# A hybrid decoder step on one core: tokens scaled when their pieces begin, four weight chunks in the idle ring, constants and counts in another order, 8 pieces ahead

## The chip, the core and the metric

The kernel runs on one core of one Trainium2 chip. The metric is the device time of one execution in microseconds; the median of several executions is compared. All data are 32-bit floats.

## What is computed

The reference is one inference step of a one-layer decoder for 1024 prompt tokens and 8 sample tokens of width 1024. Cut to what matters here:

```python
def step(y, pos):                                   # y: (tokens, 1024)
    qr, kr, vr, gr, qs, ks, vs = split(rms_norm(y, norm1_g) @ w_in)   # w_in: 1024 x 2816
    o_ret, state = retention(rotate(qr, pos), rotate(kr, pos), vr)    # 4 heads, blocks of 128 tokens, carried state
    o_swa = sliding_attention_with_sinks(qs, ks, vs)                  # 8 heads, window 128
    h = y + concat(norm(o_ret) * silu(gr), o_swa) @ w_out             # 1024 x 1024
    x = rms_norm(h, norm2_g)
    s = (x @ peer_w_q) . sub_keys                   # 8 heads x 2 halves x 128 keys
    idx, gates = top 16 of the 16 x 16 sums of the two top 16s, softmax
    a = gelu(peer_u[idx] . x) * gates               # 128 rows of 1024 per token
    return rms_norm(h + a @ peer_v[idx], final_g)
```

Each of the 1032 tokens takes 128 rows of `peer_uv`, a table of 16384 rows of 8 KB (u and v side by side). Fetching them is most of what the kernel moves: 1032 x 128 x 8 KB is 1.08 GB.

## The kernel before

**Blocks and ticks.** The 1024 prompt tokens are 8 blocks `b` of 128. For each block a loop of 128 units (`TICKS`) fetches one row per token and unit: GpSimd issues an indirect DMA (`fetch`, L577) of 1 MB into one of 8 slots of `ring`; VectorE forms the dot product with the token (`expert_dot`, L1648), ScalarE the weight (`weigh`, L1144, and scaled diagonals, L963), TensorE adds gate times row for a pair of units (`add_pair`, L899), and that frees the two slots (`used`) for the next fetches. The work for the next block ("front": `mixing`, then `picking`) is laid between these units by Python generators on each engine: each yields the tick at which its next part is due, and `advance` emits it there. Each engine runs its own list in order; only semaphores tie them.

**Ahead of the loop.** Block 0 has no loop to hide in. First `project_first` multiplies block 0 by the 8 weight chunks of `w_in` (L615), fed by `load_w` (L350) into three buffers in `ring`. Then `mixing(0)` and `picking(0)` run, with `key_weights` between them: the product of `peer_w_q` and the sub keys, from 16 loads `load_wqT` (L359), in TensorE's rows as L659. Then come the top-16 choices on VectorE (`rank`, `choose`, `number`), in two halves of the heads. `number` for a half ends with a wait for ScalarE's exponential of the gates (`best_exp`, L1115), and `move_picks` on SyncE's queue (L442, L443) then carries the choices to where GpSimd reads them. GpSimd's first fetch waits for that.

**Pieces.** The input projection of tokens 128 to 1031 is cut into 128 pieces `q` (`PIECES`): 16 column chunks for block 1, then 16 for blocks 2 and 3, then 16 for blocks 4 to 7 and the samples. A piece is `project_late` (8 matmuls, L642 and L639) on TensorE, `late_out` on ScalarE (copy with the token's scale into one of four staging places), `store_late` on SyncE (L375, 88 KB to `proj_scratch`), and `load_late` (L368, 704 KB of weights into one of three buffers, issued when the piece three chunks earlier is done). The first `AHEAD` = 14 pieces stand ahead of the loop, the others in it, at `late_tick(q)`:

```python
    if q < EARLY:
        return 1 + (q - AHEAD) * 4 // 3
```

`load_columns(b)` (L447, L448) brings a block's projected columns and its rotation table back; VectorE's `rotate` (L1311) waits for both at tick 20.

**Tokens.** The projection needs transposed tokens times the gain of the norm (`gain`, L1254), and a scale per token from its sum of squares (`count`, L1260; `load_x`, L344). Before, the transposed tokens of blocks 4 to 7 and the samples are loaded to `xT_kept` in the upper half of `ring` (L490, L492), scaled there, stored to DRAM (`xT_scratch`, L499) and loaded again in the loop (L391). The upper half of `ring` then takes `w_out` for block 0 (`wo_first`, L505).

**SyncE's queue** issues all the direct DMAs in the order written, waits included. The constants (`loads`, L494, 17 of them) stand behind all eight weight chunks and `xT_kept`.

## Time and profile before

| | us |
|---|---|
| median of 3 executions | 3050.13 |
| lowest, highest | 3045.28, 3050.16 |
| the profiled execution | 3047.14 |
| its span in the trace | 3045.3 |
| first fetch of an expert row | 200.5 |
| TensorE, VectorE, ScalarE, GpSimd busy | 74%, 67%, 34%, 39% |
| moved by the DMA engines | 1217 MB, mean 400 GB/s |

The span is read in two parts: up to the first fetch, and the loop behind it. The share of DMA is the mean busy share of the core's 16 DMA engines; GB/s says what they moved in that time, and with small packets a full share moves less.

### The profile page before, as it was taken

The page shows a single profiled execution, that of the slowest core. Times are in us where ns is not written, and L with a number is a line of the kernel's source. Part 1 is how long each engine was busy: PE and PEld are TensorE (multiplying, and loading weights), DVE is VectorE, ACT ScalarE, POOL GpSimd, SP SyncE. Part 2 cuts the span into 40 slices and gives each one's busy share as a digit, 9 for nine tenths or more (in the row PEclk, how much of TensorE's full clock was granted, in tenths as well). Part 3 has the DMA queues.
Part 4 walks back from the last instruction along what each step waited for, and adds up shares of the span by engine and source line. Part 5 has one row for each costly group of instructions (what it writes and reads, how often), then busy time and mean ns, then how long its engine had stood idle before and what let it go on. Part 6 is the DMA issues. An engine that isn't in the chain of part 4 may idle for free.

```text
span 3045.3 us, 29029 instructions
## 1 busy us (share of the span) xinstructions
PE 2251.6 (74%) x8794; PEld 961.4 (32%) x8794; DVE 2031.1 (67%) x4937; ACT 1029.3 (34%) x3215; POOL 1199.2 (39%) x1052
## 2 busy tenths in 40 slices
PE   7887968877698867866687577856785577778564
PEld 5565723544245532232222122212221122211111
DVE  2365546775468655787558865797569765886875
ACT  1322523334233343323432353233432343333322
POOL 0012343333444334434444444444444444444542
PEclk9898988998899988967798778977897789879867
DMA  8569999999999999999999999999999999999998
GB/s 312 220 244 406 403 409 416 407 421 399 421 419 419 411 416 420 417 381 411 420 421 412 407 421 421 418 403 421 421 415 408 412 418 421 408 410 421 416 408 333
DMA packets 194286, 1217.47 MB, mean 400 GB/s; under 512 B 25480, under 2 KB 44336, under 8 KB 59600
## 3 DMA queue, kind: packets, MB, share of 16 engines
q0 software_dynamic: 148608, 1082.20, 86.1%
q1 hardware_dynamic: 45520, 133.41, 11.4%
q8 instruction: 69, 1.13, 0.1%
q14 instruction: 89, 0.73, 0.1%
HBM read 1193.59 MB, written 21.54 MB: 399 GB/s over the span
## 4 chain that ended last, share of the span: by engine, by line
DMA 38%; PE 33%; DVE 16%; issue 6%; ACT 3%; POOL 3%; SPq 0%; DVEq 0%; POOLq 0%; ACTq 0%
DMA ring<-in_peer_uv,idxg 33%; PE ps L899 14%; PE ps L861 8%; DVE ring L1648 7%; PE ps L642 5%; DMA proj_scratch<-wo 3%; POOL ring L577 3%; ACT ring L963 2%; PE ps L842 1%; DMA wo<-in_w_in 1%; DVE proj L1502 1%; DVE proj L1495 1%; PE ps L659 1%; PE ps L615 1%; DVE proj L1553 1%
## 5 line engine op out<-in xcount | busy, mean ns | idle before, releaser
L577 POOL DMA_INDIRECT ring<-in_peer_uv,idxg x1024 | 1183.0, 1155 | 1607.5 <-PE ps L899 1359.2
L899 PE MATMUL ps<-ring 128*64 128x512 f32 x4096 | 1240.5, 737 | 662.2 <-ACT ring L963 660.0
L1648 DVE SCALAR_TENSOR_TENSOR ring<-ring,xlo 128x1024 f32<-128x1024 f32 x512 | 627.1, 1225 | 415.1 <-DMA ring<-in_peer_uv,idxg 400.1
L1648 DVE SCALAR_TENSOR_TENSOR ring<-ring,xhi 128x1024 f32<-128x1024 f32 x512 | 626.8, 1224 | 395.3 <-DMA ring<-in_peer_uv,idxg 384.8
L899 PEld LDWEIGHTS ps<-ring 128*64 128x64 f32 x4096 | 290.3, 158 | 1457.0 <-ACT ring L963 984.3
L1144 ACT ACTIVATE small<-small 128x2 f32<-128x2 f32 x512 | 104.7, 204 | 1638.5 <-DVE ring L1648 1627.8
L642 PE MATMUL ps<-wo 128*128 128x176 f32 x1792 | 304.1, 327 | 39.4 <-ACT wo L963 14.1
L642 PEld LDWEIGHTS ps<-wo 128*128 128x128 f32 x1792 | 279.9, 197 | 103.8 <-issue 82.3
L963 ACT ACTIVATE ring<-gdiag,small 128x64 f32<-128x64 f32 x1024 | 301.6, 342 | 16.7
L963 ACT ACTIVATE gdiag<-fold,gateg 128x64 f32<-128x64 f32 x1024 | 294.5, 336 | 1.5
L861 PE MATMUL ps<-keyw,work 128*128 128x512 f32 (+1 forms) x576 | 267.0, 608 | 1.1 <-ACT work L963 1.1
L861 PEld LDWEIGHTS ps<-keyw,work 128*128 128x128 f32 (+1 forms) x576 | 98.7, 180 | 168.3 <-issue 166.8
L1502 DVE FIND_INDEX8 proj<-proj 128x8 uint32<-128x128 f32 (+3 forms) x432 | 135.3, 333 | 0.0
L1495 DVE MAX8 proj<-proj 128x8 f32<-128x128 f32 (+3 forms) x432 | 109.5, 323 | 12.7 <-ACT proj L963 12.2
L842 PE MATMUL ps<-wo,work 128*128 128x512 f32 x224 | 109.6, 623 | 0.0
L963 ACT ACTIVATE wo<-ps,small 128x176 f32<-128x176 f32 (+2 forms) x115 | 47.9, 418 | 145.1 <-PE ps L642 78.2
L586 POOL COPY idxg<-stage 128x64 uint32<-128x64 uint32 x16 | 7.4, 461 | 199.2 <-DMA stage<-moving 199.2
L1144 ACT ACT_TABLE_LOAD x64 | 82.1, 1283 | 1.1
L1510 DVE MATCH_REPLACE8 proj<-proj 128x128 f32<-128x128 f32 (+3 forms) x216 | 66.9, 321 | 0.0
L842 PEld LDWEIGHTS ps<-wo,work 128*128 128x128 f32 x224 | 40.2, 195 | 72.0 <-issue 72.0
L1311 DVE TENSOR_TENSOR work<-proj,qsT 128x256 f32<-128x256 f32 x64 | 22.8, 421 | 55.4 <-DMA small<-in_swa_sinks 36.7
L1559 DVE TENSOR_TENSOR proj<-proj 128x256 f32<-128x256 f32 (+1 forms) x144 | 51.3, 417 | 0.1
(199 smaller groups left out, 1521.6 us busy)
## 6 DMA issues: line engine op xcount, KB each, us to landing
wo<-in_w_in SPq DMA_DIRECT2D x48, 704.0 KB
ring<-in_peer_uv,idxg POOLq DMA_INDIRECT x1024
wo<-in_w_out SPq DMA_DIRECT2D x4, 4096.0 KB, 17.5
ring<-in_w_in SPq DMA_DIRECT2D x8, 1408.0 KB, 6.9
proj_scratch<-wo SPq DMA_DIRECT2D x112, 88.0 KB
proj<-proj_scratch SPq DMA_DIRECT2D x7, 1408.0 KB
ring<-in_wqT SPq DMA_DIRECT2D x16, 512.0 KB, 7.0
h<-in_x_prompt SPq DMA_DIRECT2D x9, 512.0 KB, 9.1
```

The source lines that it names most:

```text
L577: nc.gpsimd.indirect_dma_start(row[r], None, A["peer_uv"], bass.IndirectOffsetOnAxis(ap=experts, axis=0)).then_inc(ld_row[r], 16)
L642: mm = nc.tensor.matmul(o, late_T(n, k), w[:, k, :], start=(k == 0), stop=(k == KC - 1))
L842: mm = nc.tensor.matmul(F[2 + n][0:rows, :], lhsT, weights[:, k, n * 512:(n + 1) * 512], start=(k == 0), stop=(k == KC - 1))
L861: mm = nc.tensor.matmul(F[n][0:rows, :], xT[:, k * P:k * P + rows], keyw[:, k, n * 512:(n + 1) * 512], start=(k == 0), stop=(k == KC - 1))
L899: mm = nc.tensor.matmul(acc[side * HP:(side + 1) * HP, n * 512:(n + 1) * 512], row_u[r][:, 0:HP], row_v[r][:, n * 512:(n + 1) * 512], star ...
L963: return nc.scalar.activation(o, i, ACT.Copy, **kw_)
L1144: me.did(nc.scalar.activation(gel[:, r:r + 2], dot[:, r:r + 2], ACT.Gelu))
L1495: me.did(nc.vector.max(v16(j)[:, r8 * 8:r8 * 8 + 8], rowsof(j)))
L1502: me.did(nc.vector.max_index(i16(j)[:, r8 * 8:r8 * 8 + 8], v16(j)[:, r8 * 8:r8 * 8 + 8], rowsof(j)))
L1510: me.did(nc.vector.match_replace(rowsof(j), v16(j)[:, 0:8], rowsof(j), TAKEN))
L1559: me.did(tt(o3, o3, i4[:, hh, c, :].rearrange("p (a k) -> p a k", a=1) .to_broadcast([rows, TK, TK]), ALU.mult))
L1648: ins = stt(row_u[r], row_u[r], 1.0, (xlo, xhi)[unit % 2][:], ALU.mult, ALU.mult, accum_out=dot[:, r:r + 1])
```

## The change

It does these things:

- `xT_kept`, its scaling ahead of the loop, its store and its return are gone. The tokens of blocks 4 to 7 and the samples are loaded straight from the input in the loop, twice as before, and `late_tokens` scales them on VectorE in the loop, shortly before their pieces begin; the first of these pieces move from ticks 74 and 76 to 95 and 97.
- `RESTING`: weight chunks 3 to 6 get places of their own in the upper half of `ring`, loaded after block 0 has used `w_out`. The three buffers serve the other chunks in turn. GpSimd's fifth fetch, the first into that half, waits for piece 6 and for all counts.
- All counts of later tokens stand behind the second norm of block 0, and five of their loads go to other places.
- The constants are issued before the fourth weight chunk; the first chunk is loaded and used in two halves.
- ScalarE's first exponential stands ahead of the pieces' copies; `move_picks(0, 0)` stands behind the fourth store.
- 8 pieces ahead of the loop in place of 14, the 40 others of blocks 1 to 3 at 8 per 9 ticks in place of 3 per 4.
- The rotation tables are copied once, DRAM to DRAM, beside the projected columns, and come back with them in one load.

```diff
-AHEAD = 14
+AHEAD = 8
+RESTING = (3, 4, 5, 6)
-GAP_TICKS = [74, 76, *range(95, TICKS, 2), *range(TICKS + 1, TICKS + 24, 2), TICKS + 27]
+GAP_TICKS = [*range(95, TICKS, 2), *range(TICKS + 1, TICKS + 30, 2)]
     if q < EARLY:
-        return 1 + (q - AHEAD) * 4 // 3
+        return 1 + (q - AHEAD) * 9 // 8
...
-        xT_kept = part(4 * D + KC * SPAD)
-        wbuf.append(part(KC * CW))
+        w_resting = [part(KC * LW) for _ in RESTING]
+        wbuf.append(ring[:, RING // 2 * ROWW:RING // 2 * ROWW + KC * CW])
+        x_spare = [part(D) for _ in range(2)]
...
             def load_late(l):
-                if 2 <= l < 2 * LCH:
-                    sp.wait_ge(pj_mm, NCH + (LAST_OF[l - 3] + 1 if l > 2 else 0))
+                if l in RESTING:
+                    sp.wait_ge(o_mm, 2)
+                elif 2 <= l < 2 * LCH:
+                    sp.wait_ge(pj_mm, NCH + (LAST_OF[TURNS[TURNS.index(l) - 3]] + 1 if l > 2 else 0))
...
             def load_columns(b):
                 late_stored({1: FIRST_TILE, 2: EARLY, 3: EARLY}.get(b, len(PIECES)))
-                sp.dma_start(proj[:], proj_d[b * P:(b + 1) * P, :]).then_inc(ld_proj, 16)
-                sp.dma_start(rope, A["c_rope"][b * P:(b + 1) * P, :]).then_inc(ld_proj, 16)
+                if b == 1:
+                    sp.wait_ge(st_rope, 16)
+                sp.dma_start(columns[:, 0:D_IN + 256], proj_d[b * P:(b + 1) * P, :]).then_inc(ld_proj, 16)
...
                     for unit in range(half * SLOTS // 2, (half + 1) * SLOTS // 2):
+                        if b == 0 and unit == RING // 2:
+                            hold(pool, pj_mm, NCH + LAST_OF[RESTING[-1]] + 1)
+                            hold(pool, counted, TILES)
                         hold(pool, used, b * SLOTS + (unit + 1))
...
             for q in range(AHEAD):
                 late_out(q)
-                due = advance(steps, due, 83 + q * 5 // 2)
...
+            def late_tokens():
+                for part_ in range(2):
+                    for n in range(4):
+                        yield part_ * TICKS + SKEW + PICK_AT + 19 + n
+                        if n == 0:
+                            v.wait_ge(ld_xT, 32 * (part_ + 1))
+                        gain(xT_late[:, n * D:(n + 1) * D])
+                    gain(xT_late[:, 4 * D:])
+                    me.sync()
+                    tell(xT_ready)
```

SyncE's queue before, from the third weight chunk of the projection on; `wqT` are the loads for the key weights, `in_w_in 128x1408` the weights of pieces, and the number behind x counts repeats:

```order
L350 DMA ring<-in_w_in 128x2x1408 x6
L490 DMA ring<-in_xT 128x4x1024
L492 DMA ring<-in_xT_sample 128x256
L494 DMA small<-in_c_qdec 128x4
...
L495 DMA ring<-in_sub_keysT 128x2048
L359 DMA ring<-in_wqT 128x1024 x4
L499 DMA xT_scratch<-ring 128x4352
L344 DMA xlo<-in_x_prompt 128x1024
L344 DMA xhi<-in_x_prompt 128x1024
L344 DMA gfb<-in_x_prompt 128x1024
L344 DMA g2b<-in_x_prompt 128x1024
L359 DMA ring<-in_wqT 128x1024 x2
L505 DMA ring<-in_w_out 128x8192
```

And the same stretch of the queue in the changed kernel, up to the weights of pieces:

```order
L359 DMA ring<-in_w_in 128x2x1408 x2
L495 DMA ident<-in_c_ident 128x128
L495 DMA fold<-in_c_fold 128x64
L503 DMA columns<-in_c_rope 128x256
...
L359 DMA ring<-in_w_in 128x2x1408 x5
L506 DMA ring<-in_sub_keysT 128x2048
L507 DMA wo<-in_xT 128x3x1024
L368 DMA ring<-in_wqT 128x1024 x4
L512 DMA ring<-in_w_out 128x8192
L368 DMA ring<-in_wqT 128x1024 x8
```

The constants (`c_rope` and those behind it) moved ahead of the last five chunks; the kept tokens, their store and four loads of plain tokens no longer stand between the first `wqT` loads and the fifth.

ScalarE around the pieces ahead of the loop, before; `wo<-ps` are the copies of pieces, `gates` the exponential, `gateg` the first row of the loop:

```order
L963 ACTIVATE proj<-ps 128x1024
L963 ACTIVATE wo<-ps,small 128x176 x7
L1115 ACT_TABLE_LOAD
L1115 ACTIVATE gates<-gates 128x64
L963 ACTIVATE wo<-ps,small 128x176 x7
L963 ACTIVATE gateg<-stage 128x64
```

And in the changed kernel:

```order
L980 ACTIVATE columns<-ps 128x1024
L1132 ACT_TABLE_LOAD
L1132 ACTIVATE gates<-gates 128x64
L980 ACTIVATE wo<-ps,small 128x176 x8
L980 ACTIVATE gateg<-stage 128x64
```

Seven copies no longer stand ahead of the exponential, and eight rather than seven behind it before the loop's first row.

SyncE's queue from the plain tokens of the changed kernel to the move of the first choices (`stage<-moving`):

```order
L368 DMA ring<-in_wqT 128x1024 x4
L349 DMA xlo<-in_x_prompt 128x1024
L349 DMA xhi<-in_x_prompt 128x1024
L349 DMA ring<-in_x_prompt 128x1024 x2
L379 DMA ring<-in_w_in 128x1408 x4
L349 DMA xlo<-in_x_prompt 128x1024
L349 DMA xhi<-in_x_prompt 128x1024
...
L386 DMA proj_scratch<-wo 128x176 x2
L455 DMA stage<-moving 64x64
L456 DMA stage<-moving 64x64
```

The four resting chunks stand between the first four and the last four loads of plain tokens, and the move stands behind the fourth store of a piece; before it stood behind the eighth.

## Rows read from the trace of the kernel before

**Rows 1.** The page, part 2: DMA's busy share (tenths) in 40 slices.

```profile
DMA  8569999999999999999999999999999999999998
```

**Rows 2.** Busy time by stretch: engines busy, TensorE clock, DMA share, GB/s.

```profile
0.00:200.00 200.00, 167.69 (x779) 122.42 (x780) 76.96 (x214) 50.17 (x94) 0.44 (x5) 0.94 0.66 240
125.00:173.00 48.00, 44.06 (x172) 25.17 (x170) 27.33 (x118) 11.75 (x19) 0.00 (x0) 0.93 0.15 46
173.00:200.00 27.00, 25.64 (x168) 24.83 (x167) 12.28 (x27) 5.62 (x12) 0.24 (x1) 1.00 0.83 272
200.00:3045.00 2845.00, 2083.87 (x8017) 838.95 (x8015) 1954.10 (x4723) 979.17 (x3121) 1198.75 (x1047) 0.85 1.00 411
...
302.00:390.00 88.00, 87.68 (x523) 64.70 (x521) 48.38 (x88) 46.07 (x132) 31.43 (x28) 1.00 0.98 388
```

**Rows 3.** Timeline of the first 60 us: TensorE, ScalarE, VectorE; start, duration.

```profile
10.17 40.54 PE L615 MATMUL ps<-ring,wo 128*128 128x352 f32 x128 [10.17 <-DMA ring<-in_w_in]
...
17.62 0.56 ACT L963 ACTIVATE proj<-ps,small 128x352 f32<-128x352 f32 x1 [2.12 <-PE ps L615]
...
50.75 0.55 ACT L963 ACTIVATE proj<-ps,small 128x352 f32<-128x352 f32 x1 [4.18 <-PE ps L615]
...
52.39 2.77 DVE L1311 TENSOR_TENSOR work<-proj,qsT 128x256 f32<-128x256 f32 x8 [36.70 <-DMA small<-in_swa_sinks]
...
56.84 3.00 PE L601 MATMUL ps<-ident,proj 128*128 128x128 f32 x13 [6.12 <-DVEq L1215]
```

**Rows 4.** The chain that ended last, window 0 to 420: waits for loads.

```profile
1.66 8.42 DMA ring<-in_w_in
...
72.71 21.44 DMA ring<-in_wqT
...
180.51 5.50 DMA wo<-in_w_in
...
214.25 16.45 DMA wo<-in_w_in
...
273.21 28.91 DMA proj_scratch<-wo
```

**Rows 5.** Timeline of TensorE, 90 to 216 us.

```profile
94.19 3.38 PE L659 MATMUL ps<-ring 128*128 128x128 f32 x16 [3.90 <-DMA ring<-in_wqT]
...
173.05 12.25 PE L642 MATMUL ps<-wo 128*128 128x176 f32 x80
...
217.74 1.94 PE L899 MATMUL ps<-ring 128*64 128x512 f32 x8 [1.81 <-ACT ring L963]
```

**Rows 6.** Timeline of VectorE and ScalarE, 130 to 194 us.

```profile
130.90 1.22 DVE L1260 SCALAR_TENSOR_TENSOR xlo<-xlo 128x1024 f32<-128x1024 f32 x1
...
150.02 1.02 ACT L963 ACTIVATE proj<-ps 128x1024 f32<-128x1024 f32 x1 [11.27 <-PE ps L861]
...
171.29 1.02 ACT L963 ACTIVATE proj<-ps 128x1024 f32<-128x1024 f32 x1 [13.14 <-PE ps L861]
...
180.11 0.22 DVE L1567 SCALAR_TENSOR_TENSOR proj<-proj 128x64 f32<-128x64 f32 x1
193.27 0.22 DVE L1571 TENSOR_REDUCE small<-gates 128x4 f32<-128x64 f32 x1 [12.94 <-ACT gates L1115]
```

**Rows 7.** Timeline of SyncE's queue (SPq) and GpSimd: issue times.

```profile
122.51 6.05 SPq L359 DMA_DIRECT2D ring<-in_wqT  x4
...
183.34 0.36 SPq L375 DMA_DIRECT2D proj_scratch<-wo  x1
...
194.71 0.54 SPq L442 DMA_DIRECT2D stage<-moving  x1
...
200.53 1.10 POOL L577 DMA_INDIRECT ring<-in_peer_uv,idxg  x1 [0.97 <-POOL idxg L586]
```

**Rows 8.** Timeline, 267 to 296 us: the load of block 1's columns and its wait.

```profile
267.32 0.44 SPq L447 DMA_DIRECT2D proj<-proj_scratch  x1
...
295.43 1.43 DVE L1311 TENSOR_TENSOR work<-proj,qsT 128x256 f32<-128x256 f32 x4 [17.43 <-DMA qsT<-in_c_rope]
```

More of the change, by code:

```diff
@@ L55 @@
 EARLY = LAST_OF[2 * LCH - 1] + 1
-AHEAD = 14
+AHEAD = 8
 SKEW = 12
+RESTING = (3, 4, 5, 6)
+TURNS = [l for l in range(2 * LCH) if l not in RESTING]
 HALFWAY = LAST_OF[2 * LCH + LCH // 2 - 1] + 1
@@ L499, in _ @@
-            sp.dma_start(xT_d, xT_kept).then_inc(st_xT, 16)
+            sp.wait_ge(pj_mm, NCH - 2)
+            sp.dma_start(wo_first.rearrange("p k n -> p (k n)"), A["w_out"]).then_inc(ld_wo_first, 16)
+            for n in range(4, 12):
+                load_wqT(n)
+            for dst, src in ((g2b, A["norm2_g"]), (gfb, A["final_g"])):
+                sp.dma_start(dst[:], rows_of(src, D)).then_inc(ld_gains, 16)
+            for l in range(3):
+                load_late(l)
+            load_residual(0)
@@ L500, in _ @@
+            sp.dma_start(proj_d[P:SEQ, D_IN:], A["c_rope"][P:SEQ, :]).then_inc(st_rope, 16)
+            for n in range(12, NHC):
+                load_wqT(n)
             for n in range(1, 5):
                 load_x(n)
-            for n in range(4, 6):
-                load_wqT(n)
-            sp.wait_ge(st_xT, 16)
-            sp.dma_start(wo_first.rearrange("p k n -> p (k n)"), A["w_out"]).then_inc(ld_wo_first, 16)
-            sp.dma_start(xT_early.rearrange("p (n f) -> p n f", n=3), A["xT"][1:4].rearrange("n p f -> p n f")
-                         ).then_inc(ld_xT_early, 16)
@@ L521, in _ @@
+            for n in range(5, TILES):
                 load_x(n)
@@ L523, in _ @@
                 l = PIECES[q][0]
-                if q == LAST_OF[l] and l + 3 < 2 * LCH:
-                    load_late(l + 3)
+                if l not in RESTING and q == LAST_OF[l]:
+                    load_late(TURNS[TURNS.index(l) + 3])
                 store_late(q)
-                if q == 7:
+                if q == 3:
                     move_picks(0, 0)
@@ L609, in project_first @@
                     pe.wait_ge(pj_out, c - (BANKS - 1))
-                pe.wait_ge(ld_w[c % 3], 16 * (c // 3 + 1))
+                wide = wbuf[c % 3].rearrange("p (a k n) -> p k a n", a=2, k=KC)
                 if c == 0:
                     pe.wait_ge(xT_ready, 1)
-                wide = wbuf[c % 3].rearrange("p (a k n) -> p k a n", a=2, k=KC)
+                    for a in range(2):
+                        pe.wait_ge((ld_w_half, ld_w[0])[a], 16)
+                        for k in range(KC):
+                            mm = nc.tensor.matmul(F[0][:, a * LW:(a + 1) * LW], tokens_T(0, k), wide[:, k, a],
+                                                  start=(k == 0), stop=(k == KC - 1))
+                    mm.then_inc(pj_mm, 1)
+                    return
+                pe.wait_ge(ld_w[c % 3], 16 * (c // 3 + 1))
                 for k in range(KC):
@@ L641, in project_late @@
                     else:
-                        mm = nc.tensor.matmul(o, late_T(n, k), w[:, k, :], start=(k == 0), stop=(k == KC - 1))
+                        mm = nc.tensor.matmul(o, tokens_T(n, k), w[:, k, :], start=(k == 0), stop=(k == KC - 1))
                 mm.then_inc(pj_mm, 1)
@@ L1171, in _ @@
             due, key_due = next(steps), key_tick(0)
-            for tick in range(88):
+            for tick in range(SECOND_AT):
                 due = advance(steps, due, tick)
@@ L1264, in tokens @@
             def tokens():
-                yield 11
-                v.wait_ge(ld_xT_kept, 32)
-                for n in range(4):
-                    gain(xT_kept[:, n * D:(n + 1) * D])
-                gain(xT_kept[:, 4 * D:])
-                me.sync()
-                tell(xT_ready)
-                for n in range(1, 5):
-                    yield 40 + n // 4
-                    count(n)
                 yield 42
@@ L1281, in tokens @@
                 tell(xT_ready)
-                for n in range(5, 7):
-                    yield 63
-                    count(n)
-                for n in range(7, TILES):
-                    yield 67
+                for n in range(1, TILES):
+                    yield 63 + n // 3
                     count(n)
```

96 lines of the change are left out of this document (47 added, 49 removed).

## The prediction

> **What bounds the kernel now.** I read the page's slices first: DMA stands at 9 tenths or more from the fourth slice on, and only in the first three is it lower [rows 1]. The busy time by stretch gives the sizes: from 200 us on DMA's share is 1.00 with 411 GB/s, ahead of it 0.66 [rows 2]. So behind the first fetch the time is bytes over rate, and ahead of it is a chain of dependent work with the DMA engines half idle: in 125 to 173 us their share is 0.15. No engine comes near that; TensorE's 84 us of 88 or more happens only in 302 to 390 us [rows 2], of which below. A change can therefore gain in two ways, by starting the fetches earlier (GpSimd's first at 200.53 [rows 7]) and by moving bytes from behind that point to ahead of it. Its price is whatever it moves behind it. The profiled execution took 3047.1 us for a span of 3045.3; the median of the three is 3 us above it.
>
> **The chain ahead of the first fetch**, step by step.
>
> 1. *First chunk in halves.* TensorE starts at 10.17 us, when 1408 KB have landed [rows 3, 4]. At some 420 GB/s half of it is 1.7 us less. The chunks then follow every 4.73 us ((50.75 - 17.62) / 7 [rows 3]), and the first took longer than that, 7.4 us, which I keep. -1.6 us, if the second chunk is there in time.
>
> 2. *Constants early.* VectorE waited 36.70 us for the last constant, began at 52.39, and TensorE went on at 56.84, though the last copy of the projection was done at 51.3 (50.75 + 0.55) [rows 3]. With the constants there by 20 us the rotation, 4.3 us, lies beside the later chunks. -5.4 us (56.84 - 51.3, less 0.1). The 18 issues stand ahead of the fourth chunk and take about 10 us of SyncE; the fourth chunk could not be issued before about 16 us anyway, since it waits for the first to be used, so it loses 0 to 2 us of slack that it has. I take nothing.
>
> 3. *Key weights' loads.* The chain shows 21.44 us until a `wqT` load landed at 94.15 [rows 4], and TensorE idle for 3.90 us there [rows 5]. In front of that load stood the store of 2176 KB, its 2176 KB of kept tokens, four loads of plain tokens, `w_out` and 1536 KB of early tokens. Of these `w_out` alone is left between; it is 10 us of DMA, while the fifth `wqT` load is wanted some 16 us after `w_out` is issued. -3.9 us; +-2.
>
> 4. *Counts.* VectorE's counts, 1.22 us each [rows 6], all move behind the second norm (130.9), where VectorE idles until ScalarE's score copy at 150.02. Eight are 10 us, and the room is 19. But the loads of tokens 5 to 8 stand behind four resting chunks: the last `wqT` load goes at 128.6 (122.51 + 6.05 [rows 7]), then 512 KB + 2048 KB + 2816 KB + 1536 KB at 420 GB/s, 17 us, land the last by about 147.5 with 2 us for landing. Two counts, the root and ScalarE's part end near 150.6, and ScalarE's score copy stands behind its root. +0.6 us; 0 to 5, since the sum has no slack.
>
> So the top-16 work starts 10.3 us sooner (1.6 + 5.4 + 3.9 - 0.6).
>
> 5. *The exponential.* VectorE had the first half's numbers at 180.33 and then waited 12.94 us for ScalarE [rows 6], which had seven piece copies in front. ScalarE is free at 172.3 (171.29 + 1.02), and its input is ready about then, since VectorE needs it only for the 8 us of work that end at 180.33; even an exponential of 3 us would be done in time. VectorE goes on at once and has the choices at about 181.8 (1.4 us from the exponential to the move, 193.27 to 194.71). SyncE's move now stands behind the fourth store, issued at 183.34 in before's times, so it goes at 183.5 instead of 194.71 [rows 7]. The fetch follows 5.8 us later as now. -11.2 us. The fifth fetch waits for piece 6, in before's times 190 (173.05 + 7 x 2.4 [rows 5]), and is not ready before 194. Nothing.
>
> The first fetch thus goes at 200.5 - 21.5 = 179.0 us.
>
> **What moves behind it.** At its first fetch the kernel before had issued weights up to chunk 12 and 10 stores; the changed one will have them up to chunk 9, and 4 or 5 stores. Three loads are 2.16 MB, 5.1 us. In 173 to 200 us a share of 0.83 of 27 us, 22.4 us, carried 7.3 MB [rows 2]; its nine or so landed loads take 15.5 us at 420 GB/s, which leaves about 0.6 us a store, 3.3 us for 5.5. Against this, one load of before was still under way then, -1.7 us. +6.5 us. The rotation tables cost the loop the same bytes in fewer packets, and the kept tokens come back with the same bytes: nothing, at most -1.
>
> The 10.5 us of `gain` on VectorE (8 of 1.22 us, two small) at two places in the loop stand one per unit. A unit takes 2.8 us (2845 / 1024), VectorE's own product 1.22, so they fit. Its new wait for the tokens is 7 units, 19 us, behind their issue. Nothing; up to 5 us if they land late.
>
> The 6 more pieces on TensorE are 14.5 us in a stretch where it is full: 87.68 of 88 us in 302 to 390 [rows 2]. Both sums agree there: TensorE enters the loop's first pair near 190 instead of 217.74 [rows 5] and has 14.5 us more to do, so it ends the stretch 13 us sooner if its idle time stays; DMA ends it 15 us sooner. I take the latter, since DMA's share is 1.00 over the whole loop.
>
> **Sum.** 3047.1 - 21.5 + 6.5 = 3032.1; the median stood 3.0 above the profiled execution, and I add half of that: **3033.5 us**.
>
> **A rule weighed.** Weights wait longer once the fetches run: 5.50 us before the loop, 16.45 us right behind its start [rows 4]. The Trainium skill (DMA: Bandwidth & Descriptors, Queues, rings and completion order) says that each DMA engine goes round robin between the queues that have work, packet by packet. By that alone a weight load would take about double its time alone, 11 us, and the third rival below would be nearly out. The 16.45 us disagree, being three times as long; I go by them.
>
> **The rivals.**
>
> *Weights and stores set the loop's start* (0.20). Chunks 11 to 15 serve one piece each from three buffers: three pieces per round trip of 16.45 us [rows 4], 5.5 us a piece, where the ticks want 2.9. TensorE's reserve of finished pieces is 6 smaller. If that or late counts eat 7 to 8 us of the 15: 3040.
>
> *DMA does not hold the gain back* (0.14). The stop of VectorE for block 1's columns, 17.43 us [rows 8], drained the fetches; if in the changed order it shrinks, 3 us come back, and if the bytes moved behind go into such gaps, most of the 6.5 is free: 3047.1 - 21.5 - 1 = 3024 to 3026.
>
> *Slower: the columns come later* (0.06). SyncE issues block 1's columns only when store 15 has landed. Before, it was long landed, the load went at 267.32, 67 us behind the first fetch, and came 28 us later, 95 us behind it [rows 7, 8]. Now piece 14 waits for chunk 14, that for piece 11, that for chunk 11: with a round trip R, store 15 lands about 2R + 18 behind the first fetch, and the columns 28 us after. For R = 16.45 that is 79 us, no loss. When R passes the 28.91 us that the longest store took on the chain [rows 4], it is over 104 us; from R = 32 on the stop costs more than the 15 us gained, since all fetches have landed by then and DMA idles: 3050 to 3058.
>
> *No change* (0.06). ScalarE or the new GpSimd waits bind elsewhere, and the fetches start less than 10 us sooner: 3045 to 3050.
>
> **How the numbers follow.** The forecast has 0.54; its own range is 3027 to 3038, from steps 3 and 4 at their ends. The first two rivals widen it to 3022 and 3044. The slower one and no change, 0.12 together, are left out but for their edge. A difference under 0.2%, 6 us, can't be told from none. Faster (below 3044): 0.54 + 0.14 + most of 0.20, less a little for what I have not seen, 0.83. Same 0.10, slower 0.07.
>
> **What would show it.** First fetch at 179 (174 to 185); TensorE's mixing at 50; no wait for `wqT` over 1 us; VectorE's wait for the exponential gone; the last count near 139; chunk waits of TensorE between 190 and 240 the same 15 us each; VectorE's stop for the columns 8 to 20 us; TensorE's full stretch at its end before 378 instead of 390. It is wrong if the first fetch is early and the end of that stretch is not (something in the loop's first block), or if GpSimd's fifth fetch waits.

## The result, and the profile after

The changed kernel took **3065.84 us** (median of 9 runs, 3055.72 to 3071.26), the kernel before in the same rounds 3049.17 us (9 runs, 3045.28 to 3059.43): a ratio of 1.0047, with a 95% interval of 1.0032 to 1.0063. It is slower by about 14 to 17 us where I had forecast 16 us faster. The profiled execution took 3069.5 us for a span of 3067.7 us, so it is one of the slower ones, 3.7 us above the median. The profiled execution of the kernel before stood 2.0 us below its median here. The two profiles are thus 22.4 us apart where the medians are 16.7, so some 6 us of what the traces below show as lost may be spread between executions.

The page's row of DMA's slices looks as it did in [rows 1]:

```profile
DMA  8589999999999999989999999999999999999997
```

Busy time by stretch, to set beside [rows 2], with the first fetch at 175.2 us (columns: stretch, its length, TensorE, its weight loads, VectorE, ScalarE, GpSimd, granted clock, DMA share, GB/s):

```profile
0.00:175.20 175.20, 151.02 (x733) 109.06 (x734) 72.16 (x209) 48.02 (x90) 0.47 (x6) 0.97 0.65 243
175.20:3067.70 2892.50, 2111.34 (x8080) 863.21 (x8078) 1963.19 (x4733) 976.88 (x3125) 1187.77 (x1047) 0.84 0.99 405
...
295.40:384.60 89.20, 84.35 (x498) 64.47 (x498) 39.27 (x73) 40.13 (x115) 25.74 (x24) 0.98 0.94 355
```

Ahead of the first fetch the kernel is 25 us shorter. Behind it the same loop takes 2892.5 us instead of 2844.8 (200.5 to 3045.3), at 405 GB/s instead of 411. DMA's share rounds to the same tenths in nearly every slice, which is why the first row shows nothing.

The timeline ahead of the loop, to set beside [rows 3, 5, 6, 7] (start, duration, engine, line, operation; in brackets the idle time before it and what ended it; gaps between rows are marked):

```profile
8.21 6.53 PE L626 MATMUL ps<-ring,wo 128*128 128x176 f32 x32 [8.21 <-DMA ring<-in_w_in]
...
50.16 1.61 PE L611 MATMUL ps<-ident,columns 128*128 128x128 f32 x13 [0.69 <-issue]
...
89.25 14.00 PE L859 MATMUL ps<-ring,work 128*128 128x512 f32 x32 [1.11 <-ACT work L980]
...
136.32 1.65 DVE L1498 MAX8 columns<-columns 128x8 f32<-128x128 f32 x8 [0.79 <-ACT columns L980]
...
159.73 7.43 PE L659 MATMUL ps<-wo 128*128 128x176 f32 x48
...
165.54 0.22 DVE L1574 TENSOR_REDUCE small<-gates 128x4 f32<-128x64 f32 x1
...
175.17 1.10 POOL L584 DMA_INDIRECT ring<-in_peer_uv,idxg  x1 [0.97 <-POOL idxg L593]
...
180.30 0.94 POOL L584 DMA_INDIRECT ring<-in_peer_uv,idxg  x1 [0.30 <-issue]
```

All of the front came as argued or better: TensorE starts at 8.21 and mixes at 50.16 (it was 56.84), and the wait of 3.90 us for `wqT` is gone. VectorE no longer waits for the exponential, and the fifth fetch, at 180.30, is not held. VectorE waited 6.76 us for the last four blocks of plain tokens (at 129.38); what that cost stands under the counts below. TensorE's first late piece starts at 159.73 where it started at 173.05.

**Where the lead went.** GpSimd's fetches (numbered from 0 here and below), counted in the same stretches of both kernels, show it (columns: stretch, length, GpSimd busy and number of fetches, granted clock, DMA share, GB/s). Before:

```profile
200.50:390.80 190.30, 60.20 (x56) 0.95 0.99 401
390.80:576.60 185.80, 73.56 (x64) 0.87 1.01 415
576.60:970.00 393.40, 157.36 (x137) 0.91 1.01 415
970.00:1158.00 188.00, 72.46 (x65) 0.87 1.01 415
1158.00:3045.00 1887.00, 828.03 (x712) 0.83 1.00 411
```

After:

```profile
175.10:384.60 209.50, 61.70 (x56) 0.94 0.96 374
384.60:570.40 185.80, 72.77 (x64) 0.88 1.01 415
570.40:970.80 400.40, 158.69 (x136) 0.89 0.99 405
970.80:1172.90 202.10, 72.88 (x64) 0.86 0.97 390
1172.90:3067.00 1894.10, 814.76 (x712) 0.82 0.99 409
```

The first 56 fetches take 19 us longer, the next 64 the same, the 136 behind them 7 us longer, the 64 behind those 14 us, and the last 712 another 7 us. The lead of 25.4 us at the first fetch is 6.2 us at fetch 56 and gone by fetch 160, which goes 2.6 us later than before's. So there are two questions, the start of the loop and the two places behind it.

### The profile page after: what moved, and what is told of

Read it like the earlier page. It is cut to its first block, busy times and chain, and to the rows that moved or that the text cites. A ratio compares the mean times of both kernels' runs of the same rounds, so it can differ in the third digit from the quotient of the medians.

```text
span 3067.7 us, 29063 instructions
## 1 busy us (share of the span) xinstructions
PE 2262.4 (74%) x8810; PEld 972.3 (32%) x8810; DVE 2035.3 (66%) x4942; ACT 1024.9 (33%) x3215; POOL 1188.2 (39%) x1052
## 4 chain that ended last, share of the span: by engine, by line
DMA 38%; PE 34%; DVE 14%; issue 6%; ACT 4%; POOL 3%; SPq 1%; POOLq 0%; DVEq 0%; ACTq 0%
DMA ring<-in_peer_uv,idxg 31%; PE ps L916 15%; PE ps L878 7%; DVE ring L1651 7%; PE ps L659 6%; DMA proj_scratch<-wo 5%; POOL ring L584 3%; PE ps L859 2%; ACT ring L980 2%; DVE columns L1505 1%; DVE columns L1556 1%; DMA wo<-in_w_in 1%; PE ps L676 1%; DVE columns L1498 1%; PE ps L632 1%
## 5 line engine op out<-in xcount | busy, mean ns | idle before, releaser
L916 PE MATMUL ps<-ring 128*64 128x512 f32 x4096 | 1242.2, 738 | 661.9 <-ACT ring L980 660.8
L916 PEld LDWEIGHTS ps<-ring 128*64 128x64 f32 x4096 | 291.1, 158 | 1458.8 <-ACT ring L980 987.2
L878 PE MATMUL ps<-keyw,work 128*128 128x512 f32 (+1 forms) x576 | 268.8, 611 | 1.1 <-ACT work L980 1.1
L878 PEld LDWEIGHTS ps<-keyw,work 128*128 128x128 f32 (+1 forms) x576 | 99.7, 182 | 170.0 <-issue 168.5
L1505 DVE FIND_INDEX8 columns<-columns 128x8 uint32<-128x128 f32 (+3 forms) x432 | 135.0, 328 | 0.0
L1498 DVE MAX8 columns<-columns 128x8 f32<-128x128 f32 (+3 forms) x432 | 109.4, 321 | 1.3 <-ACT columns L980 0.8
L859 PE MATMUL ps<-wo,work 128*128 128x512 f32 x224 | 108.9, 619 | 0.0
L1513 DVE MATCH_REPLACE8 columns<-columns 128x128 f32<-128x128 f32 (+3 forms) x216 | 66.8, 319 | 0.0
L859 PEld LDWEIGHTS ps<-wo,work 128*128 128x128 f32 x224 | 40.0, 194 | 73.2 <-issue 73.2
L1314 DVE TENSOR_TENSOR work<-columns 128x256 f32<-128x256 f32 x64 | 22.8, 420 | 44.5 <-DMA columns<-proj_scratch 38.5
L1562 DVE TENSOR_TENSOR columns<-columns 128x256 f32<-128x256 f32 (+1 forms) x144 | 51.4, 417 | 0.1
## 6 DMA issues: line engine op xcount, KB each, us to landing
columns<-proj_scratch SPq DMA_DIRECT2D x7, 1536.0 KB, 12.8
```

The costliest lines, as they stand in the source:

```text
L859: mm = nc.tensor.matmul(F[2 + n][0:rows, :], lhsT, weights[:, k, n * 512:(n + 1) * 512], start=(k == 0), stop=(k == KC - 1))
L878: mm = nc.tensor.matmul(F[n][0:rows, :], xT[:, k * P:k * P + rows], keyw[:, k, n * 512:(n + 1) * 512], start=(k == 0), stop=(k == KC - 1))
L916: mm = nc.tensor.matmul(acc[side * HP:(side + 1) * HP, n * 512:(n + 1) * 512], row_u[r][:, 0:HP], row_v[r][:, n * 512:(n + 1) * 512], star ...
L1498: me.did(nc.vector.max(v16(j)[:, r8 * 8:r8 * 8 + 8], rowsof(j)))
L1505: me.did(nc.vector.max_index(i16(j)[:, r8 * 8:r8 * 8 + 8], v16(j)[:, r8 * 8:r8 * 8 + 8], rowsof(j)))
L1513: me.did(nc.vector.match_replace(rowsof(j), v16(j)[:, 0:8], rowsof(j), TAKEN))
```

## The second and third place: what stands around the columns

The waits of both kernels over the whole span (engine, tile, line; what was waited for: us in total, times, longest). Before:

```profile
ACT wo L963 <- DMA proj_scratch<-wo: 62.1, 28, 7.2
...
DVE work L1311 <- DMA qsT<-in_c_rope: 18.7, 2, 17.4
...
PE ps L642 <- ACT wo L963: 14.1, 8, 4.4
```

After:

```profile
ACT wo L980 <- DMA proj_scratch<-wo: 152.8, 34, 17.1
...
PE ps L659 <- ACT wo L980: 45.7, 14, 10.3
DVE work L1314 <- DMA columns<-proj_scratch: 38.5, 3, 13.3
```

A chain of waits has grown: a store lands late, so ScalarE can't put the next piece in its place, so TensorE can't free its bank. VectorE now waits for the columns of three blocks, 12.3, 12.8 and 13.3 us; before it was 17.4 us for block 1 and 1.3 for block 2. I tried three explanations for it.

**Row pitch of the scratch.** The rows of the scratch are now 12288 B apart; another pitch might spread better.

```diff
-proj_d = nc.dram_tensor("proj_scratch", [NTOK, D_IN + 256], F32).ap()
+proj_d = nc.dram_tensor("proj_scratch", [NTOK, D_IN + 512], F32).ap()
...
```

> The changed kernel with rows of the projected columns in DRAM at a pitch of 13312 bytes (13 KB) in place of 12288 (12 KB); nothing else differs. Theory P (the pitch of 12288 makes the stores of pieces and what is read back slower, so copies on ScalarE wait for their staging places and the fetches lose their lead): ScalarE's waits for stores fall from 152.8 us in all to about 65 as before the change, and the time to 3032 +-6. Theory D (the pieces are too dense, 40 in 45 ticks, whatever a store costs): the waits stay over 120 us and the time stays near 3062.

Measured: 3066.22 us, ratio to before 1.0055 (1.0038 to 1.0072), ScalarE's waits for stores 155.1 us. The reverse, the kernel before with the pitch of 12288 B (`D_IN + 256`; the loads still take the first 11264 B of a row):

> The kernel before with the same rows at a pitch of 12288 bytes in place of 11264; the loads take the first 11264 bytes of each, all else is as before. Theory P: ScalarE's waits for stores rise from 66.6 us to over 110, the time by 10 to 25 us, in the stretches with pieces (fetches 0 to 56, 120 to 200 and 256 to 320). Theory D: no difference, within 3 us of before.

Measured: 3048.92 us, ratio 1.0001 (0.9992 to 1.0011), waits 48.1 us. The pitch is nothing.

**One load for columns and rotation table.** The kernel before with the tables copied behind the rows and read back with them:

```diff
-sp.dma_start(proj[:], proj_d[b * P:(b + 1) * P, :]).then_inc(ld_proj, 16)
-sp.dma_start(rope, A["c_rope"][b * P:(b + 1) * P, :]).then_inc(ld_proj, 16)
+sp.dma_start(columns[:, 0:D_IN + 256], proj_d[b * P:(b + 1) * P, :]).then_inc(ld_proj, 16)
...
```

> The kernel before, with the rotation tables copied once behind the columns of the scratch rows and read back with them in one load per block, as the changed kernel does. Theory R (the one load waits behind more and lands later, since nothing of a block can start before all of it is there): VectorE waits longer for the columns of blocks 2 and 3, 5 us or more in all are lost at fetches 120 to 200 and 256 to 320, and the time is 3055 or more. Rivals G and T: the load takes as long as before, 3046 to 3053.

Measured: 3047.45 us, ratio 0.9987 (0.9978 to 0.9996). The changed kernel with this undone:

> The changed kernel, with columns and rotation table loaded apart again, as in the kernel before. Theory R: VectorE's two waits of 13 us for the columns of blocks 2 and 3 go, and the time falls by 8 us or more, to 3057 or less. Rivals G and T: the waits stay at 10 to 15 us each, 3062 to 3069.

Measured: 3072.6 us, ratio 1.0073 (1.0059 to 1.0086). One load is no cause of the loss; by the medians it is a gain, 2 us in the one kernel and 7 us in the other.

**The slots of the third pass.** The change also writes the table `GAP_TICKS` anew, which my prediction had left out. The kernel before with this line alone:

```diff
-GAP_TICKS = [74, 76, *range(95, TICKS, 2), *range(TICKS + 1, TICKS + 24, 2), TICKS + 27]
+GAP_TICKS = [*range(95, TICKS, 2), *range(TICKS + 1, TICKS + 30, 2)]
```

> The kernel before, with the pieces of the third pass over the weights in the changed kernel's slots: from slot 95 in every second one up to slot 157, in place of two at 74 and 76, the rest from 95 and the last at 155. Nothing else is changed. Theory G (the later and denser slots put the last pieces, their stores and their weights around the loads of block 2's and 3's columns): the fetches up to number 112 stay at their times, between 120 and 200 some 8 us are lost, between 256 and 320 some 10 us, and the time is 10 to 20 us above the kernel before's, 3060 to 3070. Rival T (the tokens that VectorE scales in the loop) and rival R (columns and rotation table in one load): this edit has neither, no fetch moves by more than 2 us, 3046 to 3053.

Measured: **3079.79 us**, ratio 1.0093 (1.0079 to 1.0108), 30 us slower by one line, twice what I had expected. Its waits:

```profile
ACT wo L963 <- DMA proj_scratch<-wo: 115.3, 27, 19.9
...
PE ps L642 <- ACT wo L963: 49.9, 14, 14.1
DVE work L1311 <- DMA qsT<-in_c_rope: 46.5, 3, 15.8
```

These are the changed kernel's waits, in the kernel before. The opposite, the changed kernel with slots almost as before:

```diff
-GAP_TICKS = [*range(95, TICKS, 2), *range(TICKS + 1, TICKS + 30, 2)]
+GAP_TICKS = [82, 84, *range(95, TICKS, 2), *range(TICKS + 1, TICKS + 24, 2), TICKS + 27]
```

> The changed kernel, with the pieces of the third pass almost in the slots of the kernel before: the first two at slots 82 and 84 (not 74 and 76, since VectorE scales the tokens at 76 to 79), the last at 151 and 155. Theory G: VectorE's waits for the columns of blocks 2 and 3 shrink from 13 us to 5 or less, most of the 15 us lost at fetches 256 to 320 and half of the 8 us at 120 to 200 come back, 3047 to 3058. Rivals T and R: no more than 4 us come back, 3062 to 3069.

Measured: 3050.65 us, ratio 1.0009 (0.9995 to 1.0023), 15 us less than the changed kernel; VectorE waits once for columns, 14.0 us, for block 1. I call this the run with early slots.

**Why two slots cost so much.** SyncE issues in order. Its row near block 2's columns, before (start, duration of the issue):

```profile
651.43 0.33 SPq L368 DMA_DIRECT2D wo<-in_w_in  x1
...
654.30 0.47 SPq L447 DMA_DIRECT2D proj<-proj_scratch  x1
```

And after, with what VectorE and ScalarE did:

```profile
662.09 0.33 SPq L379 DMA_DIRECT2D wo<-in_w_in  x1
...
663.77 0.75 SPq L462 DMA_DIRECT2D columns<-proj_scratch  x1
...
679.59 1.43 DVE L1314 TENSOR_TENSOR work<-columns 128x256 f32<-128x256 f32 x4 [12.78 <-DMA columns<-proj_scratch]
...
682.19 0.41 ACT L980 ACTIVATE wo<-ps,small 128x176 f32<-128x176 f32 x1 [16.51 <-DMA proj_scratch<-wo]
```

Columns and moves are asked for at tick 142, counted from the start of the block before (14 ticks into the next). Each weight load is asked for one tick after the last piece of the chunk that it replaces and waits until TensorE is done with it; that piece stood at tick 137 and stands now at 141, so the load too comes up at 142, ahead of the columns. It waits there, 10.2 us for TensorE, and the moves and the 1536 KB of columns stand behind it: 9.5 us later by the clock, though the fetches were still 4.4 us ahead of before's at fetch 140. The stores of three pieces then stand behind the columns in the same queue, and ScalarE waits 16.51 us for one of them. What the stop does to the fetches comes 20 us later, as the ring runs dry (stretches of the changed kernel):

```profile
660.00:680.00 20.00, 12.56 (x80) 7.43 (x78) 4.11 (x8) 2.45 (x9) 7.74 (x8) 0.92 1.00 401
680.00:700.00 20.00, 15.84 (x90) 11.80 (x92) 14.97 (x31) 7.49 (x26) 5.91 (x4) 0.82 0.85 336
```

The test leaves the pieces in their late slots and asks for the weight loads of the third pass one tick later, in the changed kernel. One load of each half changes places with the columns by it; the others keep their order and come up a tick later, so a small part of the effect could be theirs:

```diff
 if l > l0 + 1:
-    yield late_tick(LAST_OF[l - 2]) + 1
+    yield late_tick(LAST_OF[l - 2]) + 2
 load_late(l)
```

> The changed kernel, with SyncE's weight loads of the third pass one tick later, so that the load that waits for the piece of tick 141 stands behind the moves and the columns of the next block and no longer ahead of them (the pieces keep their late slots). Theory C (the late slots cost what they do because the columns' load stands behind that wait): the columns are issued some 8 us earlier against the fetches, VectorE's waits for the columns of blocks 2 and 3 fall from 13 us to under 5, and 8 to 15 us of the loss come back, 3050 to 3058. Rival D (the number of pieces, stores and weights around the columns costs it, whoever is first in SyncE's row): the waits of ScalarE for stores stay near 150 us, and the time is 3061 to 3068.

Measured: **3049.75 us**, ratio 0.9999 (0.9986 to 1.0012): 16 us back by one character. SyncE's row and the waits of this run:

```profile
648.37 0.47 SPq L462 DMA_DIRECT2D columns<-proj_scratch  x1
656.29 0.34 SPq L379 DMA_DIRECT2D wo<-in_w_in  x1
```

```profile
ACT wo L980 <- DMA proj_scratch<-wo: 130.2, 37, 10.2
...
DVE work L1314 <- DMA columns<-proj_scratch: 14.8, 1, 14.8
```

ScalarE still waits 130 us for stores, so the sum of those waits, which had drawn my eye first, is mostly harmless. The columns are issued 15.4 us sooner, and two of VectorE's three waits are gone, those of blocks 2 and 3; the 14.8 us are block 1's. The same edit on the kernel before with the late slots:

> The kernel before with the changed kernel's late slots, which alone made it 30 us slower (3079.8), and with the weight loads of the third pass one tick later, so that the columns go first. If the wait ahead of the columns is what the slots cost, most of the 30 us come back: 3048 to 3058. If half of it is something else (three more pieces behind the block's start), 3062 to 3070.

Measured: 3062.0 us, ratio 1.0033 (1.0021 to 1.0045). Of the 30 us, 18 come back (3079.8 to 3062.0), near the changed kernel's 16; VectorE's waits for columns fall from 46.5 to 19.5 us. That is less than the first case said (3048 to 3058) and the lower end of the second. The other 10 us (3051.6 in these rounds) stay with the late slots, and which pieces cost them isn't taken apart.

**Early slots have a price too.** In the run with early slots, two pieces of each half stand at 82 and 84, among the score products (L878), the stretch that TensorE fills. Its timeline there:

```profile
858.44 1.94 PE L916 MATMUL ps<-ring 128*64 128x512 f32 x8
...
863.85 2.55 PE L659 MATMUL ps<-wo 128*128 128x176 f32 x16
866.33 1.94 PE L916 MATMUL ps<-ring 128*64 128x512 f32 x8
```

From one pair of units (L916) to the next it is 7.9 us with a piece and 5.5 us without (874.21 to 879.71). Two pieces are 4.8 us, and this run loses just that against the kernel before between fetches 90 and 100, and again between 216 and 232. I tried to put them elsewhere:

```diff
-GAP_TICKS = [*range(95, TICKS, 2), *range(TICKS + 1, TICKS + 30, 2)]
+GAP_TICKS = [95, 96, 97, 98, *range(99, TICKS, 2), *range(TICKS + 1, TICKS + 24, 2), TICKS + 27]
```

> The changed kernel, with the first four pieces of each half of the third pass in slots 95 to 98 (two behind each other at a time), the next ones in every second slot, so that the last stand at 151 and 155 as in the kernel before, and none stands among TensorE's score products. If the two pieces at slots 82 and 84 cost the run with early slots 2.4 us each in the stretch that TensorE fills (3.63 + 1.87 us of every 5.5), this one comes out 3 to 8 us below it: 3042 to 3048. If the pairs bring ScalarE's waits for stores there (four places for pieces), it is 3050 to 3056.

Measured: 3056.26 us, ratio 1.0022 (1.0009 to 1.0034), just above the second case. Fetches 104 to 110 come 12 us later there: with pieces back to back ScalarE waits 10.4 us for a store, TensorE 4.35 us for ScalarE, and GpSimd once 10.5 us for TensorE. Four places for pieces don't bear pieces in a bunch.

## The first place: how the loop starts

**The exponential alone.** The kernel before with the first exponential ahead of the pieces and the first move behind the fourth store (`if q == 3` for `if q == 7` on SyncE, `range(SECOND_AT)` for `range(88)` on ScalarE):

> The kernel before with only the first exponential ahead of the pieces' copies and the move of the first choices behind the fourth store. By the prediction's step 5 and its ledger the first fetch comes 11 us sooner and the time falls by 5 to 9 us, since 5 loads of weights and 5 stores move behind it. If an earlier first fetch is worth nothing (the loop's first block is bound by TensorE's pieces): within 2 us of before.

Measured: 3054.3 us, ratio 1.0019 (1.0008 to 1.0029). The first fetch went at 192.3, 8 us sooner, and fetch 56 at 398.6, 8 us **later**. TensorE's timeline shows why; its pieces now wait for weights while the fetches are under way:

```profile
206.92 5.06 PE L642 MATMUL ps<-wo 128*128 128x176 f32 x16 [4.22 <-DMA wo<-in_w_in]
...
231.90 1.94 PE L899 MATMUL ps<-ring 128*64 128x512 f32 x8 [1.80 <-ACT ring L963]
```

It reaches the first pair at 231.90, before at 217.74 [rows 5]. Ahead of that pair it waits for weights five times, 12.5 us in all; in the kernel before it was 5.0 us in three waits. The fetches had taken their lead from the weights of the 14 pieces that stand ahead of the first pair.

**Fourteen pieces ahead in the changed kernel.**

```diff
-AHEAD = 8
+AHEAD = 14
-        return 1 + (q - AHEAD) * 9 // 8
+        return 1 + (q - AHEAD) * 4 // 3
```

> The changed kernel with 14 pieces ahead and the spacing of 3 per 4 ticks as before, the pitch of 12288 kept. Theory P: fetches 0 to 56 still lose, the time stays within 8 us of the changed kernel (3058 to 3070), since the losses at fetches 120 to 200 and 256 to 320 have no part in this. Theory D: the loss in the first 56 fetches goes, 3045 to 3052.

Measured: 3062.45 us, ratio 1.0043 (1.0027 to 1.006), 3.4 us less. Fetch 56 is 10.9 us ahead of before's and not 6.2. Neither number is beyond the noise by itself: the two intervals overlap. The rest of the loss, which I had hoped to find here, stayed. With the early slots:

> The changed kernel with the early slots (82, 84, 95 and on) and 14 pieces ahead of the loop as in the kernel before. The changed kernel with 14 pieces alone was 3.4 us faster than the changed kernel. If the two causes are apart, they add: 3045 to 3049. If the lead is lost in any case at the first TensorE-bound stretch, it is as with the early slots alone, 3049 to 3053.

Measured: 3047.16 us, ratio 0.9996 (0.9987 to 1.0006), 3.5 us less than with eight pieces, as if the causes add. And with the exponential late again, at eight pieces and early slots:

> The changed kernel with the early slots, and with the first exponential back behind seven piece copies and the first move behind the eighth store: the first fetch goes some 8 us later, near 186, while all that stands ahead of it stays as early as in the changed kernel. Theory F (the first fetches only swap places with the weights that the pieces of the loop's start need, so their lead is worth nothing): from fetch 32 on no fetch is more than 3 us later than with the early slots alone, and the time is 3047 to 3053. Rival, by the prediction (an earlier first fetch passes its lead on to the end): 8 us slower, 3056 to 3060.

Measured: 3058.43 us, ratio 1.0031 (1.0018 to 1.0044), **8 us slower** than the run with early slots, by the medians, and 14 us later at fetch 56. My theory, that the lead of the first fetch is worth nothing, fell here. TensorE's timeline of this run tells the difference to the kernel with fourteen:

```profile
199.09 3.68 PE L916 MATMUL ps<-ring 128*64 128x512 f32 x8 [16.21 <-ACT ring L980]
```

Its eight pieces end at 181, and it idles 16.21 us until the first rows are there. The new theory: TensorE's row from its first late piece decides the first stretch. A fetch that comes sooner helps only as far as TensorE would have nothing to do. Two runs with fourteen pieces and columns first test it, the exponential early and late:

> The changed kernel with the columns of a block ahead of the weight load (as in the run with SyncE's loads one tick later) and with 14 pieces ahead of the loop. If TensorE's row from its first late piece on decides the first stretch, fetch 56 goes 217 to 219 us behind that piece, 12 to 14 us sooner than in the kernel before, and 5 us of it more than with 8 pieces reach the end: 3042 to 3047, the fastest of all. Rival: the lead runs out in the later blocks in any case (DMA's bytes), 3048 to 3052.

> The same with the first exponential behind seven piece copies and the first move behind the eighth store, as in the kernel before. The first fetch goes 8 to 11 us later, near 185. Theory E (TensorE's row decides, and with 14 pieces it has work until then): fetch 56 comes no more than 2 us later than in that run, or even sooner by up to 5 us, as the kernel before lost 5.4 us by the early exponential; the time is 3038 to 3048. Rival (the fetches' lead counts by itself, as it did with 8 pieces): 8 us slower, 3051 to 3056.

Measured: **3045.07 us**, ratio 0.9980 (0.9969 to 0.9991), and **3044.69 us**, ratio 0.9975 (0.9966 to 0.9985); the kernel before took 3051.61 in these rounds. Eight us of lead at the first fetch (177.5 or 185.5) make no difference. Busy time from TensorE's first late piece to fetch 56, in the same columns as above, for the kernel before, exponential early and exponential late:

```profile
173.05:390.83 217.78, 189.91 (x1085) 144.78 (x1085) 120.92 (x302) 76.91 (x224) 60.44 (x58) 0.95 0.97 384
```

```profile
162.02:379.38 217.36, 189.78 (x1085) 145.75 (x1085) 119.39 (x297) 75.79 (x224) 62.79 (x58) 0.96 0.94 371
```

```profile
159.99:376.91 216.92, 192.20 (x1085) 147.16 (x1085) 120.94 (x302) 76.69 (x224) 59.29 (x57) 0.94 0.95 373
```

The same 1085 matrix products take 217 us in all three, whether the first fetch comes 27.5, 15.5 or 25.5 us behind the start of the stretch. One run with fourteen pieces does not fit, the kernel before with the exponential alone (first fetch 17 us behind the start):

```profile
175.31:398.59 223.28, 192.24 (x1085) 146.28 (x1085) 121.08 (x302) 75.85 (x224) 63.76 (x57) 0.94 0.95 376
```

So the rule is one of the changed kernel, whose weight chunks 3 to 6 rest in places of their own and can be loaded ahead; that this is the difference is not tested. With eight pieces and the exponential late it is another picture:

```profile
161.80:396.80 235.00, 194.44 (x1085) 148.63 (x1085) 119.07 (x297) 75.80 (x224) 60.95 (x57) 0.92 0.89 344
```

The changed kernel itself lies between, here beside the run with pieces in a bunch, whose program is the same up to fetch 56:

```profile
159.73:384.63 224.90, 194.67 (x1085) 149.36 (x1085) 119.51 (x297) 75.11 (x224) 61.93 (x57) 0.95 0.93 360
```

```profile
157.54:376.74 219.20, 192.04 (x1085) 145.63 (x1085) 120.75 (x301) 75.04 (x224) 59.81 (x58) 0.95 0.94 369
```

One profile of each says little about a few us here. The six traces with eight pieces and an early exponential give 219.2 to 224.9 us and fetch 56 4.4 to 14.1 us ahead of before's; the four of the changed kernel with fourteen pieces give 216.9 to 218.7 us and 10.9 to 13.9 us. Fourteen are better on the mean, by some 4 us, and the changed kernel's own trace is the worst of the six.

## Why the prediction was wrong

**Right: the chain ahead of the first fetch.** Forecast 179.0, measured 175.17, and its signs were there (the last count came 4 us before the time given; the sign of the full stretch's end follows below). *First chunk in halves* was 2.0 us at TensorE's start (8.21 against 10.17), forecast 1.6. *Constants early* and the halves together gave 6.7 us at TensorE's mixing (50.16), forecast 7.0. *Key weights' loads* and what hangs on them gave 10.8 us where I had 3.9: TensorE's L859 starts 17.4 us sooner, of which 6.7 were there at the mixing. TensorE's busy time between the two points, before and after, says what I left out:

```profile
56.84:106.69 49.85, 39.14 (x245) 36.30 (x245) 22.05 (x40) 24.49 (x50) 0.00 (x0) 0.84 0.75 295
```

```profile
50.16:89.25 39.09, 31.48 (x245) 28.84 (x245) 15.96 (x31) 24.24 (x50) 0.00 (x0) 1.00 0.63 240
```

The idle time fell by 3.1 us (10.7 to 7.6), about what I had forecast. The same 245 products were 7.7 us shorter, since TensorE's granted clock was 1.00 in place of 0.84: before, the engine had idled 6.12 us ahead of the mixing, and its next products (59.63 to 63.15 us) ran at 0.54, nearly all of it the lower of the two levels, 1.2 GHz. After, it idled 0.69 us there. My sum had no term for the clock. *Counts* cost 2.6 us (the `MAX8` is 14.8 us sooner, L859 17.4), forecast 0.6, with the last count at 134.7 and not 139. The 6.76 us that VectorE waited for plain tokens lie in that stretch. *The exponential* gave 10.6 of the 11.2: 25.4 us at the first fetch less the 14.8 that were there at the `MAX8`.

**Wrong: the step from the first fetch to the end.** The prediction's own sign of being wrong came up: the first fetch was early, and TensorE's full stretch ended at 384.6 and not before 378. The step that failed is the sentence "I take the latter, since DMA's share is 1.00 over the whole loop", with the "Nothing" for the loop behind it. I had both sums on paper, TensorE's 13 us and DMA's 15, and treated them as agreeing, while they were two different bounds with different starts. By it, 15 of the 21.5 us gained ahead of the loop were to reach the end; the trace has 25.4 us of lead at the first fetch, and at fetch 1023 the kernel is 20 us behind. Three things failed in it.

1. *TensorE's start is the lead, not the first fetch's.* Its first late piece comes 13.3 us sooner, so some 13 us can reach fetch 56; the exponential, half of my forecast gain, isn't part of that. The runs with fourteen pieces got 11 to 14 us there, the changed kernel 6.2 us, other runs with its first stretch 4.4 to 14.1. My condition "if its idle time stays" was the right one, but nothing in the text checked it: TensorE's idle time in this stretch was 27.9 us before (217.78 less 189.91) and 30.2 us after (224.90 less 194.67), and it was busy 4.8 us longer with the same number of products. The eight pieces cost 3.4 to 4.7 us of the end by the medians of three pairs of runs; in each pair the intervals overlap, and only the three together show it.

2. *The slots of the third pass were left out.* The diff shows the table and the prediction doesn't name it. Against almost the old slots it costs 15 us in the changed kernel, and that decides the sign. With the columns ahead of the weight load the kernel is level with the one before (3049.75 us): so this order explains the loss of 16 us, and the forecast gain of 16 us is still missing behind it, most of it in the first stretch, where the lead of that run goes from 22.9 us to 7.4. The mechanism is nearly my slower rival's (columns that come late and a ring that runs dry), but in blocks 2 and 3, where I had not looked, and by another cause: not a late store, but a weight load ahead of the columns in SyncE's row. I had priced the rival's stop for block 1, where it didn't change (12.3 us against 17.43 in [rows 8]).

3. *The ledger of moved bytes* was about right in bytes (1171.4 MB behind the first fetch against 1169.6, from each page's total less 243 GB/s times 175.2 us and 239 times 200.5) and says little. By it the loop would have been 4 us longer; it is 48 us longer. Its sum in the prediction is slightly off as well: 5.1 + 3.3 - 1.7 is 6.7 and not 6.5; and 8 pieces per 9 ticks of 2.8 us want one each 3.1 us, where the first rival has 2.9. Neither matters to the outcome.

The tokens scaled in the loop, which I had costed at nothing, can't be read off alone: no run takes them out. The run with early slots loses, from fetch 56 to the end, just the two 4.8 us, which leaves little room for them; the same with fourteen pieces loses 7 us more than that between fetches 56 and 1023, in a profile that is its slowest execution (3053.1 us). But they are what holds the slots 74 and 76 closed, since VectorE scales these tokens at 76 to 79, and so they push two pieces per half into TensorE's score products or to the end.

**What stays open.** The best version is ahead by 11.4 us at fetch 56 (exponential early) and by 5.0 at the last one of a prompt token. Some of it goes between fetches 256 and 450, in steps of 1 to 2 us that differ from run to run (the profiled executions of one kernel vary by several us, 3041 to 3052 in that one's runs), and I can't put a name to them. The 10 us that the late slots cost the kernel before beyond the columns are shown as a sum and not placed. Why TensorE's first late piece comes at 157.5 to 162.2 us in four traces of programs that are the same up to there is open too; that is as much as the number of pieces is worth.

## What to carry to other kernels

A DMA share of 1.00 over a loop doesn't turn a lead at its start into a lead at its end: follow one counter, here the fetch number, through both kernels, since a mean share of 0.99 beside 1.00 stood over a loop that took 48 us longer. In a queue that issues in order, ask of each large load that an engine will wait for what stands directly ahead of it and for which event that waits; a step of four slots in the table was worth 16 us, and one tick on the other load gave it back. And before an earlier transfer is counted as a gain, find the engine that works through the first stretch and see whether it is idle there: with fourteen pieces of other work ahead, 8 us of lead at the first fetch were worth nothing (in the kernel before they cost 4.5 us), and with eight pieces 10 us of lead were worth 8. And where a change takes waits from TensorE, read its granted clock on both sides: here 7.7 of 10.8 us gained were clock.

## What the runs showed of the hardware

DMA engines at a full share don't move bytes at one rate: before, it was 422 GB/s between 250 and 275 us and 392 GB/s between 200 and 225, both with a share of 1.00 or more, and the run with columns first, fourteen pieces and the late exponential had 1.00 with 391 GB/s in its TensorE-bound stretch. By the page of the kernel before, part 3, the fetches moved 1082 MB in 86.1% of the engines' time and SyncE's transfers 133 MB in 11.4%: 7% less per time. A store of a piece writes 128 rows of 704 B, where a fetched row is 8 KB; that this is why is likely and not tested. I had made the ledger with one rate. And a load of 704 KB for the pieces ahead of the loop is slowed at once by the fetches under way (in the run with the exponential alone TensorE waited 4.22 us for one chunk).

The changed kernel's chain has a weight load of 16.20 us at 210.07 us, near the 16.45 us of [rows 4]. This is what the DMA queues of the kernel before did while the latter was under way, 214.3 to 230.7 us (packets, MB, share of the 16 engines; q0 has the fetches, q1 SyncE's transfers):

```profile
q0 software_dynamic: 696, 5.07, 73.6%
q1 hardware_dynamic: 690, 1.84, 27.9%
```

The two queues take turns packet for packet: 696 to 690 here, 1155 to 1155 between 250 and 275 us, 695 to 690 in the changed kernel's 210.1 to 226.3. The Trainium skill (DMA: Bandwidth & Descriptors, Queues, rings and completion order) has each DMA engine go round robin between the queues by packets, and these counts agree with it. So the prediction was wrong to say that the 16.45 us disagree with that rule. It had read equal turns as equal bytes. A packet of the fetches is 7.3 KB here and one of SyncE's queue 2.7 KB, so that queue got 27% of the bytes and not half, and it moved 1.84 MB in this time, more than the one load of 0.72. Its starting point was off as well: 704 KB at 422 GB/s would take 1.7 us (an estimate from this trace's rate), so the 5.50 us of [rows 4] weren't one load's time alone.
